# First modulation blocks cut by outputs, first two projections cut by slices of k, and attention scores two units ahead

## The reference, cut to what matters

```
c_act = jax.nn.silu(c)
mod = c_act @ ada_w[l] + ada_b[l]
sh_m, sc_m, g_m, sh_f, sc_f, g_f = jnp.split(mod[:, None, :], 6, axis=-1)
h = _rmsnorm(x, norm_mix[l]) * (1 + sc_m) + sh_m
proj = h @ w_in[l]
qa, ka, va, cq, ckv, kr, z, xbc, dt_raw, gates = jnp.split(proj, _IN_OFFSETS, axis=-1)
```

## Time and profile before

| | |
|---|---|
| median of 3 runs | 1951.82 us (1950.03 to 1952.05) |
| the profiled execution | 1946.01 us |
| its span, first to last instruction | 1944.2 us |
| mean granted TensorE clock | 0.983 |
| TensorE busy | 1864.6 us, 96% |
| VectorE, ScalarE busy | 32%, 22% |
| DMA | 443.25 MB, 228 GB/s over the span |

### The profile page before, as it was taken

How to read it: one execution, slowest core, us unless ns; L and a number is a source line. 1 busy time by engine, 2 the same in 40 slices (tenths; PEclk the granted TensorE clock), 3 DMA queues, 4 the chain that set the end, 5 groups by cost and what they waited for, 6 DMA issues and landing times.

```text
span 1944.2 us, 20225 instructions
## 1 busy us (share of the span) xinstructions
PE 1864.6 (96%) x8628; PEld 1304.4 (67%) x8628; DVE 628.2 (32%) x1139; ACT 418.7 (22%) x888; POOL 0.8 (0%) x9
## 2 busy tenths in 40 slices
PE   6999999999999999999999999999889999999996
PEld 2477787888888648788888888865764444444432
DVE  4352267333232335127642232034441111111112
ACT  3253122212110234312212111012421011011112
POOL 0000000000000000000000000000000000000000
PEclk8999999999999999999999999999989999999999
DMA  9753364264446665337245453453329999999993
GB/s 388 266 168 125 130 218 154 105 216 156 147 161 229 215 216 174 130 111 274 92 161 185 132 171 136 141 216 130 135 82 406 428 428 427 427 427 427 428 427 128
DMA packets 137433, 443.25 MB, mean 228 GB/s; under 512 B 8832, under 2 KB 58240, under 8 KB 123520
## 3 DMA queue, kind: packets, MB, share of 16 engines
q1 hardware_dynamic: 134912, 438.26, 59.6%
q10 hardware_dynamic: 2432, 3.71, 0.6%
HBM read 440.11 MB, written 1.84 MB: 227 GB/s over the span
## 4 chain that ended last, share of the span: by engine, by line
PE 91%; DVE 4%; ACT 2%; DMA 1%; issue 1%; DVEq 1%; PEldq 0%; SPq 0%; ACTq 0%; PEld 0%
PE acc L705 36%; PE acc L1147 11%; PE acc L715 10%; PE aux L1186 6%; PE aux L980 4%; PE acc L980 4%; PE acc L1134 3%; PE acc L1001 3%; PE acc L1195 2%; PE aux L641 2%; PE aux L1195 2%; DMA ring<-in_ada_first 1%; PE acc L956 1%; PE aux L651 1%; PE aux L804 1%; ACT area L1269 1%
## 5 line engine op out<-in xcount | busy, mean ns | idle before, releaser
L705 PE MATMUL acc<-hT,ring 128*128 128x256 f32 x2688 | 592.2, 382 | 7.1 <-ACT hT L1342 7.1
L705 PEld LDWEIGHTS acc<-hT,ring 128*128 128x128 f32 x2688 | 513.2, 192 | 80.6 <-issue 12.0
L715 PE MATMUL acc<-ring,hT 128*128 128x512 f32 (+1 forms) x384 | 165.5, 591 | 5.3 <-ACT hT L1342 5.3
L1147 PE MATMUL acc<-ring,yT 128*64 128x512 f32 x512 | 169.2, 594 | 0.0
L2098 DVE SCALAR_TENSOR_TENSOR area<-acc,vectors,area 128x255 f32<-128x255 f32 (+1 forms) x176 | 72.7, 476 | 214.1 <-ACT area L1522 212.5
L715 PEld LDWEIGHTS acc<-ring,hT 128*128 128x128 f32 x384 | 73.7, 194 | 90.6 <-issue 88.4
L2336 DVE TENSOR_TENSOR xT<-xT,acc 128x1024 f32<-128x1024 f32 x17 | 20.8, 1222 | 292.3 <-PE acc L1195 292.3
L1724 DVE SCALAR_TENSOR_TENSOR ring<-ring,cspread 128x1024 f32<-128x1024 f32 x80 | 93.2, 1221 | 63.3 <-DMA ring<-in_ada_rest 63.3
L1147 PE MATMUL acc<-area,yT 128*64 128x512 f32 x384 | 112.9, 594 | 0.0
L1147 PEld LDWEIGHTS acc<-ring,yT 128*64 128x64 f32 x512 | 52.4, 137 | 74.5 <-issue 74.5
L1269 ACT ACTIVATE area<-aux 128x512 f32<-128x512 f32 (+3 forms) x65 | 41.4, 676 | 230.7 <-PE aux L641 225.1
(11 more groups left out here) (379 smaller groups left out, 1951.8 us busy)
## 6 DMA issues: line engine op xcount, KB each, us to landing
ring<-in_w_in SPq DMA_DIRECT2D x34, 2048.0 KB, 9.6
ring<-in_ffn_w_up SPq DMA_DIRECT2D x44, 1024.0 KB, 7.7
ring<-in_ada_rest SPq DMA_DIRECT2D x20, 2048.0 KB, 8.0
ring<-in_w_up SPq DMA_DIRECT2D x17, 2048.0 KB, 18.8
ring<-in_w_down SPq DMA_DIRECT2D x17, 2048.0 KB, 18.4
ring<-in_w_gate SPq DMA_DIRECT2D x16, 2048.0 KB, 15.6
area<-in_w_up SPq DMA_DIRECT2D x12, 2048.0 KB, 19.2
area<-in_w_down SPq DMA_DIRECT2D x12, 2048.0 KB, 17.8
```

The source lines that it names most:

```text
L705: mm = pe.matmul(acc[LU.buf[use]][:, SEQ * j:SEQ * j + SEQ], w[:, k, c0:c0 + P], x[:, k, :], start=(k == 0), stop=(k == n - 1))
L715: mm = pe.matmul(acc[LU.buf[use]][:, at:at + width], x[:, k, P * t:P * t + P], w[:, k, :], start=(k == 0), stop=(k == n - 1))
L1147: mm = pe.matmul(dst[CAP * e:CAP * e + CAP, :], xg[:, b, k, CAP * e:CAP * e + CAP], w[:, k, :], start=(k == 0), stop=(k == KT - 1))
```

## The change

The 2048 columns of `ada_first` are packed anew: block i now holds all rows of the 512 columns that give shift and scale of tiles k = 2i and 2i + 1, as 16 KB in each partition. So the first block gives two whole tiles of h. The loads are issued in the order block 0, q, block 1, k, block 2, block 3, into slots 0, 2, 1, 3, 0, 1; block 2 waits for block 0 to be used, and so on. q and k leave the list of chunks, v and ada4 are put ahead.

TensorE follows an order written out by hand: each block, its sums, bias groups, and quarters of q and k, a quarter being the two tiles of one block for both token tiles. Each block's sums are drained, copied by VectorE, folded, and made into gains for its two tiles (`first_gains`); ScalarE shifts those two tiles (`first_shift`). The bias groups go to `aux`, the sums of squares to `acc[1]`. The counts of `acc_free` start at 0. The loads of `rows` and `cspread` are issued after the second shift.

In the second block's attention TensorE makes the scores of u + 2 behind the transposes of u, and VectorE finds the maximum of u + 1 ahead of its wait for the exponentials of u.

More of the change, by code:

```diff
@@ L195, with __init__ @@
 class Use:
-    def __init__(self, names, first=(0, 0), free=(1, 1)):
+    def __init__(self, names, first=(0, 0), free=(0, 0)):
         self.buf, self.full, self.turn = {}, {}, {}
@@ L650, in norm_sum @@
                         pe.wait_ge(x_sq, 2 * before + k // 2 + 1)
-                    mm = pe.matmul(aux2[:, 0:SEQ], ones, squared[:, k, :], start=(k == 0), stop=(k == KT - 1))
+                    mm = pe.matmul(dst[:, 0:SEQ], ones, squared[:, k, :], start=(k == 0), stop=(k == KT - 1))
                 mm.then_inc(x_ss, 1)
-            norm_sum(0)
-            early = acc[0][:, 0:512]
+            norm_sum(0, dst=acc[1])
             def bias_group(g):
@@ L666, in bias_group @@
                         mm.then_inc(bias_full, 1)
-            pe.wait_ge(c_ready, 1)
[L669 to L679, removed]
+            def first_block(i):
[7 more added lines that the diff above has]
+                pe.drain().then_inc(early_full, 1)
@@ L680, in _ @@
+            first_block_sums(3)
[4 more added lines that the diff above has]
+            first_quarter("k", 3)
             pe.wait_ge(kc_in, 16)
[L681 to L684, removed]
             for l in range(DEPTH):
@@ L1287, in _, with take_bias, first_shift @@
             act.activation(cact, vectors[:, X_C:X_C + KT], ACT.Silu).then_inc(c_silu, 1)
-            act.dma_start(rows.rearrange("p l n -> p (l n)"), a["spread"].to_broadcast([P, DEPTH * R_END])).then_inc(rows_in, 16)
[L1289 to L1294, removed]
+            act.wait_ge(x_ss, 1)
+            root(rstd, acc[1][:, 0:SEQ], D, (x_rt, 1))
+            def take_bias(g):
+                act.wait_ge(bias_full, 2 * g + 2)
+                copy(bias1[:, g, :] if g < 4 else bias0[:, g - 4, :], aux[:, 512 * (g % 2):512 * (g % 2) + 512]).then_inc(bias_out, 1)
+            def first_shift(i):
+                for k in (2 * i, 2 * i + 1):
+                    act.wait_ge(h_scaled, k + 1)
+                    act.activation(hT[:, k, :], hT[:, k, :], ACT.Identity, bias=mod[:, k:k + 1]).then_inc(h_ready, 1)
+            take_bias(0)
[4 more added lines that the diff above has]
+            first_shift(1)
+            act.dma_start(rows.rearrange("p l n -> p (l n)"), a["spread"].to_broadcast([P, DEPTH * R_END])).then_inc(rows_in, 16)
+            act.dma_start(cspread, a["c"].to_broadcast([P, D])).then_inc(c_in, 16)
[3 more added lines that the diff above has]
+            take_bias(5)
             for l in range(DEPTH):
@@ L1790, in mix_gains @@
                 def mix_gains():
-                    if l == 0:
-                        dve.wait_ge(ada_done, 1)
-                    tt(mod[:, 0:16], (modr if l else pmod)[:, 0:16], cc[:, V_ADA:V_ADA + 16], ALU.add)
+                    tt(mod[:, 0:16], modr[:, 0:16], cc[:, V_ADA:V_ADA + 16], ALU.add)
                     D_()
@@ L2189, in take_linear, with largest @@
                 dve.tensor_copy(dst[:, j0:j0 + 2, :], shaped(pmod, 2, SEQ)).then_inc(t2_out, 1)
-            for u in range(8):
+            def largest(u):
                 b, t = u % 2, u // 2 % 2
```

57 lines of the change are left out of this document (22 added, 35 removed).

## The result

The changed kernel takes 1966.65 us (median of 4 runs, 1965.72 to 1967.12) against 1951.34 of before in the same comparison (4 runs): ratio 1.0087, 95% interval 1.0072 to 1.0102. It is slower, as forecast, but by 15.3 us between the medians, three times the forecast's 5.0, and lies above the range, which ended at 1962. Its profiled execution took 1965.72, its span is 1963.9: 19.7 more than the span of before. Executions of before took from 1944.68 to 1952.48 us, at mean granted clocks of 0.984 to 0.978, and the profiled one is among the quicker, which is why 19.7 stands beside 15.3. The sum is checked on the two spans.

What follows compares the result with a forecast made beforehand. Expert stage bound by its loads, starting when TensorE's chain arrives; v late by 5.9 plus 1.7 clock, attention -2.6, sum +5.0 on 1946.0, plus 5.8 to the median: 1956.8 us, range 1951.3 to 1962.

Steps and rivals of the forecast that it cites:

- B: Opening: the moment TensorE ends bias group 5, between q3 and k3, forecast at 64.0 us.
- from B to v: ScalarE's queue after bias group 5: bias copy 0.7, DMA issues 7.6, copies and squares 2.1; v starts at 74.4.
- half clock at v: Start of v: after TensorE stands for 7.0 us the clock is not granted in full, costing 1.7 us.
- attention, to the transposes of unit 7: Second block's attention: four shorter rounds save 3.6, squares cost 1.5, a copy wait 0.5; -2.6 us.
- q0 comes at full clock as I count it: Opening: q's first quarter runs at full rate, 3.44 us, from 23.0 to 26.4.
- From there it is dense: Opening: from q1's start at 35.3 TensorE works without a break for 17.0 us, to 52.3.
- rival (c): Opening: the clock falls there too, one or two losses of 1.7 us; sum +6.7 to +8.4, chance 0.17.
- What is late next: Between q3 and v: ScalarE's work queued behind bias group 5 delays freeing q's accumulator; v 5.9 us late.
- rival (b): ScalarE's queue before v: short DMA issues, v starts at 72.4, sum +3.0, 1954.8 us, no change; chance 0.23.
- Rival (a): Opening: VectorE does not hold TensorE up, bias group 5 ends near 55.4; faster, 1946 us; chance 0.10.
- Rival (d): ScalarE before v: a table change costs more than its load, v 1.9 us later, sum +6.9, 1958.7; chance 0.05.
- The edits costed at nothing: Repacked `ada_first` rows, moved `rows` and `cspread` loads, ada6 ahead of uqkv, ada5's timing: claimed to cost nothing.

Runs made afterwards that it cites:

- tables_first: Changed kernel with ScalarE's Silu, exponentials and sines put ahead of its copy of bias group 5: 1963.57 us, 1.0081 of the kernel before.
- step7_early: Changed kernel with VectorE's step 7 made while TensorE is at block 1, so bias group 3 need not wait: 1959.74 us, 1.0055 of the kernel before.
- open_filled: Changed kernel with useless matmuls filling four TensorE waits in the opening, no wait removed: 1965.74 us, 1.0086 of the kernel before.
- tables_copies: Changed kernel with ScalarE's tables and functions ahead of bias group 5's copy, and q and k copies ahead of the eight DMA issues: 1953.94 us, 1.0022 of before.
- mid_half_filled: Kernel before with the new attention order and useless matmuls (two, one, three) in TensorE's waits at units 6 and 7: 1944.2 us, 0.9984 of before.
- opening_only: Changed kernel's new opening with the old order of the second block's attention: 1969.91 us, 1.0108 of the kernel before.
- open_mended: Changed kernel with tables and copies moved forward, step 7 early, two shift pairs ahead of bias copies, and filling matmuls ahead of q0: 1945.85 us, 0.9983 of before.
- copies_first: Changed kernel with ScalarE's copies and squares of q and k put ahead of the eight DMA issues: 1961.95 us, 1.0073 of the kernel before.

## Why the prediction was wrong, step by step

The sum, term by term (us, against before):

| term | forecast | measured |
|---|---|---|
| B, end of bias group 5 | 64.0 | 70.5 |
| from B to v | 10.4 | 14.2 |
| v against 68.53 | +5.9 | +16.2 |
| half clock at v | +1.7 | +1.8 |
| ml to the first scores | 0 | +0.3 |
| attention, to the transposes of unit 7 | -2.6 | -2.5 |
| clock at units 6 and 7 | 0 | +2.1 |
| to the first expert | 0 | +0.25 |
| last expert | 0 | +1.65 |
| sum | +5.0 | +19.7 |

- **The step that failed first: "then the DMA issues ... 7.6 in all ... the engine's own three tables and functions take 42.10 to 47.73, 5.6; I take the longer".** They are not two alternatives. The issues do run ahead of the sines, but not of Silu, the first table and the second: 45.77 is 3.67 behind 42.10 in the earlier trace rows itself, and 74.84 is 3.67 behind 71.17 after. The tail is 3.67 + 7.6, and `tables_first` gave 3.4 of it back. The row that showed it stood in the document.
- **B = 64.0.** The waits were right (bias group 3 waits 2.59, forecast 2.7), and so were the rates. What failed is "q0 comes at full clock as I count it" and "From there it is dense": q0 lost 1.6 (5.07 for 3.44) and q1 with k0 3.1 (9.97 for 6.88); of the rest of the 6.5, 0.9 is bias group 1, also at half clock (1.93 for 1.06), and the remainder gaps of 0.2 to 0.3 between the stretches. That is rival (c), given 0.17, with more than its 3.4. `step7_early` and `open_filled` show the cause: q1 and k0 run at full rate with the wait for step 7 taken away, and q0 too with the waits filled. The rule of the Trainium skill (TensorE: Matmul & The Clock Gate, Loop structure matters more than you think), that matmuls with waits for transfers between them run cold, gave the right sign for both q0 and q1, though the waits here, 1.2 to 2.6 us, were mostly for VectorE and ScalarE. I had set against it a block that ran at full rate behind one wait; it is no evidence for several waits in a row.
- **What is late next** (bias group 5, the tail, q's accumulators, v) was right in kind: `tables_copies` removes it whole, 12.7 us. As the eight issues again took 7.6, rival (b) falls.
- **Half clock at v:** right, 1.8 for 1.7.
- **Attention:** -2.6 was right up to unit 7's transposes. The prediction took TensorE's times there from rows at full clock and put nothing for the clock in this stage; that step failed: behind the wait of 1.11 ahead of unit 6's transposes the clock was at half, and 2.1 was lost. Filling the waits gives it back (`mid_half_filled`: 3.4 won). Before pays some of this as well, but later: its clock is at half from 1391, in the last transposes, and with the same old order `opening_only` has it already in unit 7's values. What decides where the clock falls is not settled.
- **Rival (a)** fell with B: even `open_mended` ends bias group 5 at 62.2, not below 57. **Rival (d)** fell: each function starts 0.01 behind its table, as before. The Trainium skill (ScalarE: Activation LUTs, What ACT_TABLE_LOAD costs) counts 2.66 us for a switch; the trace has 1.28 in every row here.
- **The edits costed at nothing** show 0.3 between ml and the first scores, less than the 1.2 by which unchanged code differs there.
- **The time added to the sum.** The forecast put 5.8 between the profiled execution and the median, as in before; in after it is 0.9 (1966.65 - 1965.72). So the time of 1956.8 misses by 9.9, but the sum by 14.7: that the time came nearer is luck.

## What to carry to other kernels

When a step is moved behind another, move its whole queue with it: take the distance from the first instruction of the tail to the last from the trace as one piece, and don't replace a serial stretch by the longer of two parts. Where an order puts matmuls between waits, allow for half clock behind each group of waits (here 1.6 us in q0, 3.1 in q1 and k0), and where a round of TensorE's work gets shorter than what another engine needs, the gain can be paid back in clock unless the wait is filled (here 2.1 of 2.5 us). ScalarE work whose inputs are ready belongs in front of a wait, and copies that free an accumulator in front of DMA issues.

## What the runs showed of the hardware

- A wait of 1.23 ahead of q1 left the clock full when little idle time stood ahead of it (`step7_early`: 7.11 for two quarters), and not when a wait of 2.59 did (9.97). Matmuls of no use in the waits kept the granted clock at 1.00 from 14 to 66 us (`open_filled`).
- The eight issues took 7.9 us where they began at 72.1 (`tables_first`), 7.6 at 74.8 (after) and 6.5 at 75.8 (`opening_only`); with copies of q and k queued ahead of them (`copies_first`), the first began beside the copies (76.07, the first copy 76.29) and the copies were not held up.
- The half clock in the last expert: 1.5 to 1.7 us in all twelve changed kernels, in neither profiled execution of before.
